# A whole down projection in three passes of fp32r, contiguous expert down weights, and pad slots left out of the scatter-add

## The chip, the cores and the metric

The kernel runs on one core of one Trainium2 chip. The metric is the device time of one execution in microseconds (us); the profile is one profiled execution.

## The reference

One layer of a streaming encoder in float32, over 1024 prompt tokens and 64 sample tokens (N = 1088 rows of width D = 1024):

```python
h   = rmsnorm(x, g0) * (1 + sc_m) + sh_m          # adaLN modulation from c @ w_ada
mix = concat(pool_mixer(u), window_attention(q, k, v)) @ w_out
x   = x + gt_m * rmsnorm(mix, g1)
h   = rmsnorm(x, g2) * (1 + sc_f) + sh_f
# 64 experts of width 256, each token goes to 6 of them, weighted
y   = sum_e w_e * ((silu(h @ w_gate[e]) * (h @ w_up[e])) @ w_down[e])
y  += (silu(h @ ws_gate) * (h @ ws_up)) @ ws_down # shared expert
x   = x + gt_f * rmsnorm(y, g3)
```

The outputs are x and the last rows of the pooling, key and value states.

## The kernel before

The first 560 us do the mixing sub-layer, the shared expert and the routing. The routing gives each expert a list of slots, cut into tiles of 128 slots; the last tile of an expert is filled up with pad slots. There are 1088 x 6 = 6528 real slots. The run had 83 tiles (each has one `y_of` on ScalarE, L1047) for 64 experts, so 19 tiles are a second tile of an expert; `ftab` marks the first tile of an expert, `etab` names the expert. Below, a tile whose step rounds new weights is called a fresh one.

Every engine walks over the tiles in a loop of its own, written out by hand (`tile(i, odd)`), and they meet at semaphores. What each does in step i:

- **SyncE** loads expert weights into a ring of four slots: gate and up (1 MB each, in two halves) as soon as the last tile of the expert four back has been through gate and up, down (1 MB) as soon as that tile has been through the down projection. It issues gate and up of an expert only after the ones before have landed; the down load of the expert before is then still in flight. A partition's half row of gate or up is 4 KB in one piece, and down is 4 KB rows, two per partition.
- **GpSimd** gathers the rows of h of tile i+3 from `h2_rows` by index (`gather`, L771; pad slots hold the index N + r, which is out of bounds, and are skipped), then adds the weighted results of tile i-1 to `y_acc` in HBM with an accumulating indirect DMA (`scatter_add`, L779). It waits for the scatter-add before it (`added`), since two tiles may hold the same token. Pad slots add into the P spare rows N to N+127 of `y_acc`.
- **ScalarE**: SiLU of the gate (L1062), copy of the transposed x rounded to fp32r (`xt_copy`, L1002), in a fresh tile rounding of the next expert's gate and up to fp32r (`round_next`, L983, two of 128x2048), `y_of(i-1)` (L1047, which also needs `slot_columns`), copy of the transposed activations as plain f32 (`at_copy`, L1042).
- **VectorE**: product of SiLU and up (`act_of`, L1389), what rounding left over of x (`xt_rest`, L1398), three index columns (L1407, L1402, L1403; before L1402 it waits until the scatter-add of tile i-3 has landed), in a fresh tile what rounding left over of gate and up (`rests`, L492, two of 128x2048), written over the raw weights in the ring.
- **TensorE**: transposes of the activations of tile i-1 (`act_t`, L1760, 2 instructions), gate and up of tile i in three passes of fp32r (`expert_in`, L1669 to L1671, 24 matmuls of 512 columns), transposes of x of tile i+1 (`x_t`, L1749, 8), down projection of tile i-1 in plain f32 (`expert_out`, L1770: 4 matmuls of 512 columns, each of which stands as two instructions).

The shared expert already does its down projection in three passes of fp32r with the helper `swiglu_out` (12 matmuls of 512 columns). After the last scatter-add, `y_acc` is read back, normalised, and added.

## Time and profile before

| | |
|---|---|
| time, median of 3 runs | 1466.43 us (1465.84 to 1475.8) |
| profiled execution | 1465.69 us, of which span 1463.9 us |
| mean granted TensorE clock | 0.977 of full speed |
| busy | PE 91%, VectorE 54%, ScalarE 45%, GpSimd 26% |
| moved by DMA | 352.38 MB; queue q1 (SyncE) 279.39, q0 (GpSimd) 72.38 |
| expert stage | from 560 us to the last scatter-add's landing at 1430 us |

The span runs from the first to the last instruction; the profiled execution is 1.8 us longer. q0 carries the gathers and the scatter-adds, q1 the weights. The share of a DMA queue is the time of its packets as a share of 16 DMA engines. "SPq" is SyncE's queue, "PEld" TensorE's weight load. In a timeline a row has the start, the duration, engine, line, operation and, in brackets, the idle time before it and what ended it.

### The profile page before, as it was taken

How to read it: one execution, taken by the hardware profiler on the slowest of the kernel's cores; microseconds unless marked ns; L12 is line 12 of the kernel's file. 1: busy time of each engine (PE TensorE's matmuls, PEld its weight loads, DVE VectorE, ACT ScalarE, POOL GpSimd, SP SyncE). 2: the span in 40 equal slices, each digit the busy share in tenths (PEclk: the TensorE clock that was granted, in tenths of full speed). 3: DMA queues.
4: the chain of work that ended last, by engine and by line, in shares of the span. 5: the costliest groups of instructions: out<-in, count | busy, mean ns of one | idle time of the engine just before them, and what ended most of it. 6: DMA issues, size and time to landing. Idle time of an engine off the chain costs nothing.

```text
span 1463.9 us, 22685 instructions
## 1 busy us (share of the span) xinstructions
PE 1338.2 (91%) x5590; PEld 882.4 (60%) x5591; DVE 794.7 (54%) x1254; ACT 656.7 (45%) x916; POOL 387.2 (26%) x274
## 2 busy tenths in 40 slices
PE   4999997899998989999999999999999999999950
PEld 1467654545455766766666666776667667667630
DVE  2446676835887634555546454465545345555426
ACT  2300005734435335555555454465555345555523
POOL 3000000003565431233333323243222333232330
PEclk9999999999999999999999999999999999999995
DMA  8925424032221626999999999999999989999977
GB/s 303 347 79 184 143 69 120 1 145 86 87 90 42 223 88 227 343 324 322 358 310 307 349 318 358 295 311 326 362 324 317 261 225 275 290 338 322 315 193 254
DMA packets 106744, 352.38 MB, mean 241 GB/s; under 512 B 16369, under 2 KB 18517, under 8 KB 106356
## 3 DMA queue, kind: packets, MB, share of 16 engines
q1 hardware_dynamic: 79864, 279.39, 52.8%
q0 software_dynamic: 26560, 72.38, 21.3%
q8 instruction: 19, 0.31, 0.1%
q10 hardware_dynamic: 284, 0.16, 0.1%
q14 instruction: 17, 0.14, 0.0%
HBM read 307.15 MB, written 62.83 MB: 253 GB/s over the span
## 4 chain that ended last, share of the span: by engine, by line
PE 39%; DMA 37%; DVE 9%; SPq 5%; issue 4%; ACT 3%; POOL 2%; ACTq 0%; POOLq 0%; DVEq 0%
DMA raw<-in_w_up_dram 25%; DMA y_acc<-arena,idxs 8%; PE ps L1529 7%; PE ps L1770 7%; PE ps L1669 4%; PE ps L1671 4%; PE ps L1670 4%; SPq L582 3%; PE ps L1622 3%; DMA arena<-in_w_ada_dram 2%; PE ps L1474 2%; DMA y_acc<-arena 2%; PE ps L1749 2%; SPq L649 1%; PE ps L1534 1%
## 5 line engine op out<-in xcount | busy, mean ns | idle before, releaser
L492 DVE TENSOR_TENSOR lo_ring<-raw,hi_gate_up (+1 forms) x128 | 287.7, 2289 | 166.5 <-ACT hi_gate_up L983 156.6
L1770 PE MATMUL ps<-raw,aT 128*128 x664 | 301.9, 598 | 19.3 <-ACT aT L1042 17.0
L983 ACT ACTIVATE hi_gate_up<-raw (+1 forms) x128 | 238.1, 1908 | 120.4 <-SPq L663 93.5
L779 POOL DMA_INDIRECT y_acc<-arena,idxs x83 | 152.2, 1834 | 522.8 <-DMA y_acc<-arena,idxs 389.6
L1669 PE MATMUL ps<-hi_gate_up,xTh 128*128 x664 | 266.3, 401 | 1.1 <-issue 1.1
L1671 PE MATMUL ps<-hi_gate_up,xTl 128*128 x664 | 259.5, 391 | 0.0
L1670 PE MATMUL ps<-lo_ring,xTh 128*128 x664 | 259.0, 390 | 0.0
L1770 PEld LDWEIGHTS ps<-raw,aT 128*128 128x128 f32 x664 | 120.2, 191 | 142.9 <-issue 142.8
L771 POOL DMA_INDIRECT arena<-h_rows,idxg x86 | 114.8, 1334 | 100.0 <-DVE idxg L1407 77.0
L1671 PEld LDWEIGHTS ps<-hi_gate_up,xTl 128*128 128x128 f32 x664 | 124.7, 188 | 26.9
L1669 PEld LDWEIGHTS ps<-hi_gate_up,xTh 128*128 128x128 f32 x664 | 124.8, 188 | 24.5 <-issue 1.2
L1670 PEld LDWEIGHTS ps<-lo_ring,xTh 128*128 128x128 f32 x664 | 125.0, 188 | 23.7
L1398 DVE TENSOR_TENSOR xTl<-ps,xTh 128x1024 fp32r<-128x1024 f32 x84 | 102.7, 1223 | 66.4 <-ACT xTh L1002 66.2
L1529 PE MATMUL ps<-arena 128*128 128x384 f32 (+1 forms) x432 | 135.8, 476 | 1.1 <-DVE arena L1138 1.1
L1622 PE MATMUL ps<-arena 128*128 128x512 f32 (+1 forms) x288 | 128.4, 601 | 0.5 <-ACT arena L910 0.5
L1389 DVE TENSOR_TENSOR arena<-arena,ps 128x256 f32<-128x256 f32 x83 | 34.8, 419 | 166.7 <-ACT arena L1062 166.6
L1047 ACT ACTIVATE arena<-ps,wcol 128x1024 f32<-128x1024 f32 x83 | 91.3, 1100 | 58.9 <-PE ps L1770 44.3
L1062 ACT ACTIVATE arena<-ps 128x256 f32<-128x256 f32 x82 | 31.4, 383 | 189.4 <-PE ps L1671 189.3
L1529 PEld LDWEIGHTS ps<-arena 128*128 128x128 f32 x432 | 83.2, 193 | 53.0 <-issue 5.0
L750 POOL TENSOR_TENSOR arena<-arena 128x1024 f32<-128x1024 f32 (+1 forms) x9 | 22.0, 2443 | 314.8 <-DVE arena L1305 314.8
L1002 ACT ACTIVATE xTh<-ps 128x1024 fp32r<-128x1024 f32 x84 | 86.1, 1025 | 33.4 <-PE ps L1749 33.3
L1622 PEld LDWEIGHTS ps<-arena 128*128 128x128 f32 (+1 forms) x288 | 52.4, 186 | 65.4 <-issue 64.5
(244 smaller groups left out, 1457.4 us busy)
## 6 DMA issues: line engine op xcount, KB each, us to landing
raw<-in_w_gate_dram SPq DMA_DIRECT2D x128, 512.0 KB, 6.0
raw<-in_w_up_dram SPq DMA_DIRECT2D x128, 512.0 KB, 9.0
raw<-in_w_down_dram SPq DMA_DIRECT2D x64, 1024.0 KB, 11.8
arena<-in_w_ada_dram SPq DMA_DIRECT2D x32, 512.0 KB, 6.4
arena<-in_w_ada_dram SPq DMA_DIRECT2D x4, 2048.0 KB, 17.4
arena<-in_x_prompt_dram SPq DMA_DIRECT2D x16, 512.0 KB, 8.9
x_rows<-arena SPq DMA_DIRECT2D x8, 512.0 KB, 2.9
h_rows<-arena SPq DMA_DIRECT2D x8, 512.0 KB, 2.6
```

Source lines behind the costliest of these rows:

```text
L492: return eng.tensor_tensor(lo_of(e, m), raw_of(e, m), hi_of(e, m).bitcast(F32), ALU.subtract)
L771: pool.indirect_dma_start(out=xg[b], out_offset=None, in_=h2_rows, in_offset=bass.IndirectOffsetOnAxis(ap=idxg[b][:, 0:1], axis=0), bounds ...
L779: pool.indirect_dma_start(out=y_acc, out_offset=bass.IndirectOffsetOnAxis(ap=idxs[b][:, 0:1], axis=0), in_=yw[b], in_offset=None, bounds_c ...
L983: act.activation(hi_of(e, m), raw_of(e, m), ACT.Copy).then_inc(round_gu, 1)
L1047: act.activation(yw[b], pair(2), ACT.Copy, scale=wcol[b][:, 0:1]).then_inc(yw_s, 1)
L1398: dve.tensor_tensor(xTl, pair(6).rearrange("p (k n) -> p k n", k=KD), xTh.bitcast(F32), ALU.subtract)\
L1529: ins = pe.matmul(out[:, 0:n_], w1[:, k, P * c:P * (c + 1)], hT[:, k, a:a + n_], start=(k == 0), stop=(k == KD - 1))
L1622: ins = pe.matmul(bank(2 * (t % 2) + half)[0:ROWS[t], :], hT[:, k, P * t:P * t + ROWS[t]], wo[:, k, 512 * half:512 * half + 512], start=(k ...
L1669: pe.matmul(out, at_h[:, k, :], w_h, start=first, stop=False)
L1670: pe.matmul(out, at_h[:, k, :], w_l, start=False, stop=False)
L1671: return pe.matmul(out, at_l[:, k, :], w_h, start=False, stop=last)
L1770: ins = pe.matmul(bank(2 + half), aT[:, k, :], down[:, k, 512 * half:512 * half + 512], start=(k == 0), stop=(k == KF - 1))
```

## The change

Four things: the down weights are loaded as (p k) n, so that a partition holds rows 2p and 2p+1 in 8 KB without a break, and `act_of` writes its columns in the matching order (a step of two elements in both of its inputs); ScalarE rounds the down weights (`round_down`, one 128x2048 per expert, one expert ahead, behind `at_copy`) and VectorE makes their rest (`down_rest`) and the rest of the activations (`act_rest`, 128x256); `expert_out` is `swiglu_out` with 12 matmuls of fp32r and waits for both rests; the scatter-add skips indices from N on and `y_acc` keeps 2 spare rows, which two small copies at the start touch instead of 128. The semaphores of the last reads are merged with earlier ones.

```diff
-        down_v = w_down[0].rearrange("e (k p) n -> e p k n", p=P)
+        down_v = w_down[0].rearrange("e (p k) n -> e p (k n)", k=KF)
...
-            for r in (0, P // 2):
-                pool.dma_start(y_acc[N + r:N + r + P // 2, :], x_prompt[0, r:r + P // 2, :]).then_inc(added, 16)
+            for r in range(2):
+                pool.dma_start(y_acc[N + r:N + r + 1, :], x_prompt[0, r:r + 1, :]).then_inc(added, 16)
...
-                                        in_=yw[b], in_offset=None, bounds_check=add_bound,
+                                        in_=yw[b], in_offset=None, bounds_check=row_bound, oob_is_err=False,
                                         compute_op=ALU.add).then_inc(added, 16)
...
             def at_copy(i):
                 act.wait_ge(at_mm, i + 1)
-                act.activation(aT, bank(5)[:, 0:DE]..., ACT.Copy).then_inc(at_s, 1)
+                act.activation(aTh, bank(5)[:, 0:DE]..., ACT.Copy).then_inc(aeh_s, 1)
+
+            def round_down(e):
+                act.wait_ge(dn_ready, e + 1)
+                act.activation(hi_of(e, 2), raw_of(e, 2), ACT.Copy).then_inc(round_dn, 1)
+
+            def round_next_down(i):
+                f = act.value_load(ftab[0:1, bass.ds(i, 1)], min_val=0, max_val=2)
+                e = act.value_load(etab[0:1, bass.ds(i, 1)], min_val=0, max_val=NE - 1)
+                with act.If(f > 1):
+                    round_down(e + 1)
...
+            act.wait_ge(shg_mm, NT)
+            round_down(0)
             round_next(0)
             at_copy(0)
+            round_down(1)
...
                 y_of(i - 1, 1 - odd)
                 at_copy(i)
+                round_next_down(i)
...
             def act_of(i):
                 dve.wait_ge(silu_s, i + 1)
-                dve.tensor_tensor(act_m, sg, bank(4)[:, DE:2 * DE], ALU.mult).then_inc(act_s, 1)
+                def of_k(x):
+                    return x.rearrange("p (q k) -> p k q", k=KF)
+                dve.tensor_tensor(act_m.rearrange("p (k q) -> p k q", k=KF), of_k(sg), of_k(bank(4)[:, DE:2 * DE]), ALU.mult)\
+                    .then_inc(act_s, 1)
...
+            def down_rest(e):
+                dve.wait_ge(round_dn, e + 1)
+                dve.tensor_tensor(lo_of(e, 2), raw_of(e, 2), hi_of(e, 2).bitcast(F32), ALU.subtract)\
+                    .then_inc(lo_dn, 1)
...
+            def act_rest(i):
+                dve.wait_ge(aeh_s, i + 1)
+                dve.tensor_tensor(aTl, bank(5)[:, 0:DE]..., aTh.bitcast(F32), ALU.subtract)\
+                    .then_inc(ael_s, 1)
...
                 slot_columns(i - 1, 1 - odd)
                 rests(i)
+                act_rest(i)
+                next_down_rest(i)
...
             def expert_out(i, e):
                 pe.wait_ge(yw_s, i + 1)
-                pe.wait_ge(dn_ready, e + 1)
-                pe.wait_ge(at_s, i + 1)
-                down = raw_of(e, 2).rearrange("p (k n) -> p k n", k=KF)
-                for half in range(2):
-                    for k in range(KF):
-                        ins = pe.matmul(bank(2 + half), aT[:, k, :], down[:, k, 512 * half:512 * half + 512],
-                                        start=(k == 0), stop=(k == KF - 1))
-                ins.then_inc(dn_mm, 1)
+                pe.wait_ge(lo_dn, e + 1)
+                pe.wait_ge(ael_s, i + 1)
+                swiglu_out(2, aTh, aTl, hi_of(e, 2), lo_of(e, 2)).then_inc(dn_mm, 1)
```

## Rows read from the trace of the kernel before

**Rows 1.** Page of the profile, part 1: busy time, share of the span, instructions
```profile
PE 1338.2 (91%) x5590; PEld 882.4 (60%) x5591; DVE 794.7 (54%) x1254; ACT 656.7 (45%) x916; POOL 387.2 (26%) x274
```

**Rows 2.** Windows: us; busy (x count) PE PEld DVE ACT POOL; PEclk; DMA share; GB/s
```profile
560.00:1033.00 473.00, 455.37 (x1901) 318.25 (x1899) 245.83 (x299) 256.12 (x254) 148.35 (x89) 1.00 0.98 321
1033.00:1404.00 371.00, 369.88 (x1546) 259.29 (x1547) 181.99 (x236) 193.12 (x199) 110.82 (x74) 1.00 0.95 301
```

**Rows 3.** Waits, 570 to 1404 us: who waited for what, us, times, longest
```profile
POOL y_acc L779 <- DMA y_acc<-arena,idxs: 375.4, 59, 8.8
...
ACT hi_gate_up L983 <- SPq L663: 93.5, 25, 6.7
```

**Rows 4.** Timeline of TensorE: one expert tile, then the shared expert's down projection
```profile
1073.72 3.60 PE L1770 MATMUL ps<-raw,aT 128*128 x8
1077.15 0.38 PE L1760 MATMUL ps<-ident,arena 128*128 128x128 f32 x2
...
539.99 0.39 PE L1669 MATMUL ps<-hi_down,aTsh 128*128 128x512 f32 x1
...
542.48 0.39 PE L1671 MATMUL ps<-hi_down,aTsl 128*128 128x512 f32 x1
```

**Rows 5.** Timeline of ScalarE in a tile that rounds new weights
```profile
1085.59 3.72 ACT L983 ACTIVATE hi_gate_up<-raw  x2 [0.65 <-issue]
1089.22 1.09 ACT L1047 ACTIVATE arena<-ps,wcol 128x1024 f32<-128x1024 f32 x1
1090.21 0.37 ACT L1042 ACTIVATE aT<-ps 128x256 f32<-128x256 f32 x1
```

**Rows 6.** Timeline of VectorE in the same tile
```profile
1083.47 0.42 DVE L1389 TENSOR_TENSOR arena<-arena,ps 128x256 f32<-128x256 f32 x1 [7.09 <-ACT arena L1062]
1084.98 1.23 DVE L1398 TENSOR_TENSOR xTl<-ps,xTh 128x1024 fp32r<-128x1024 f32 x1 [1.09 <-ACT xTh L1002]
...
1086.24 0.14 DVE L1403 COPY idxs<-prod 128x1 int32 x1
1087.96 4.50 DVE L492 TENSOR_TENSOR lo_ring<-raw,hi_gate_up  x2 [1.57 <-ACT hi_gate_up L983]
1093.55 0.42 DVE L1389 TENSOR_TENSOR arena<-arena,ps 128x256 f32<-128x256 f32 x1 [1.09 <-ACT arena L1062]
```

**Rows 7.** Timeline of ScalarE behind a late weight load
```profile
611.36 0.37 ACT L1042 ACTIVATE aT<-ps 128x256 f32<-128x256 f32 x1
...
611.88 1.03 ACT L1002 ACTIVATE xTh<-ps 128x1024 fp32r<-128x1024 f32 x1
```

**Rows 8.** DMA queues (packets, MB, share): 317:318.5, 313.8:315.8, 961.5:962.3 twice, 1424:1430.5
```profile
q1 hardware_dynamic: 155, 0.62, 100.4%
...
q1 hardware_dynamic: 117, 0.86, 102.4%
...
DMA packets 51, 0.14 MB, mean 169 GB/s; under 512 B 18, under 2 KB 18, under 8 KB 51
...
q0 software_dynamic: 51, 0.14, 42.5%
...
q0 software_dynamic: 144, 0.52, 52.4%
```

**Rows 9.** Timeline of GpSimd's scatter-adds (loaded; weight queue silent; tail), and ScalarE's last
```profile
1055.41 1.57 POOL L779 DMA_INDIRECT y_acc<-arena,idxs  x1 [7.16 <-DMA y_acc<-arena,idxs]
...
1065.54 1.58 POOL L779 DMA_INDIRECT y_acc<-arena,idxs  x1 [7.22 <-DMA y_acc<-arena,idxs]
...
1389.78 1.58 POOL L779 DMA_INDIRECT y_acc<-arena,idxs  x1 [5.54 <-DMA y_acc<-arena,idxs]
...
1396.72 1.57 POOL L779 DMA_INDIRECT y_acc<-arena,idxs  x1 [2.27 <-DMA y_acc<-arena,idxs]
...
1424.03 1.55 POOL L779 DMA_INDIRECT y_acc<-arena,idxs  x1 [5.64 <-issue]
...
1416.59 1.11 ACT L1047 ACTIVATE arena<-ps,wcol 128x1024 f32<-128x1024 f32 x1 [6.18 <-DVE idxs L1403]
```

More of the change, by code:

```diff
@@ L98, in build @@
         slot_rows = nc.dram_tensor("slot_rows", (NE * CAP, 2), F32, kind="Internal").ap()
-        y_acc = nc.dram_tensor("y_acc", (N + P, D), F32, kind="Internal").ap()
+        y_acc = nc.dram_tensor("y_acc", (N + 2, D), F32, kind="Internal").ap()
         BIG, TR, XS, RW = RING * WSLOT, KD * N, NT * D, 4 * 2 * D
@@ L168, in build @@
         xTh, xTl = f32r_tiles("xTh", BIG + 6 * D, KD), f32r_tiles("xTl", BIG + 7 * D, KD)
-        aT = nc.alloc_sbuf_tensor_at("aT", [P, DE], F32, offset=SBUF_AT + 4 * (BIG + 5 * D + 2 * DE))[:, :]\
-            .rearrange("p (k n) -> p k n", k=KF)
+        aTh, aTl = f32r_tiles("aTh", BIG + TR + XS + 3 * D, KF), f32r_tiles("aTl", BIG + TR + XS + 3 * D + DE, KF)
         def at(a, n):
@@ L391, in build @@
         at_mm = sem("at_mm")
-        at_s = sem("at_s")
         slot_col = sem("slot_col")
@@ L396, in build @@
         added = sem("added")
-        y_in = [sem(f"y_in{t}") for t in range(NT)]
+        aeh_s = sem("aeh_s")
+        ael_s = sem("ael_s")
+        round_dn = sem("round_dn")
+        lo_dn = sem("lo_dn")
         fin_ss = sem("fin_ss")
@@ L584, in load_down @@
             def load_down(g, s):
-                src = down_v.rearrange("(g s) p k n -> s g p k n", s=RING)[s, bass.ds(g, 1)].rearrange("a p k n -> (a p) k n")
-                sp.dma_start(raw_at(2, (s + 1) % RING).rearrange("p (k n) -> p k n", k=KF), src).then_inc(dn_slot[s], 16)
+                src = down_v.rearrange("(g s) p n -> s g p n", s=RING)[s, bass.ds(g, 1)].rearrange("a p n -> (a p) n")
+                sp.dma_start(raw_at(2, (s + 1) % RING), src).then_inc(dn_slot[s], 16)
             def load_expert(g, s):
@@ L672, in _ @@
                     sp.wait_ge(dn_mm, last_of + 1)
-                sp.dma_start(x1_t(t)[0:ROWS[t], :], x1_rows[P * t:P * t + ROWS[t], :]).then_inc(y_in[t], 16)
+                sp.dma_start(x1_t(t)[0:ROWS[t], :], x1_rows[P * t:P * t + ROWS[t], :]).then_inc(x_in[t], 16)
             last = sp.value_load(lasti[0:1, NE - 1:NE], min_val=NE - 1, max_val=MAX_TILES - 1)
@@ L676, in _ @@
             for t in range(NT):
-                sp.dma_start(y_t(t)[0:ROWS[t], :], y_acc[P * t:P * t + ROWS[t], :]).then_inc(y_in[t], 16)
+                sp.dma_start(y_t(t)[0:ROWS[t], :], y_acc[P * t:P * t + ROWS[t], :]).then_inc(x_in[t], 16)
             for t in range(NT):
@@ L763, in _ @@
                 scatter_slots(t, 0, TOPK)
-            gather_bound, add_bound = pool.to_reg(N - 1), pool.to_reg(N + P - 1)
+            row_bound = pool.to_reg(N - 1)
             def gather(i, b):
@@ L772, in gather @@
                                         in_offset=bass.IndirectOffsetOnAxis(ap=idxg[b][:, 0:1], axis=0),
-                                        bounds_check=gather_bound, oob_is_err=False).then_inc(gathered[b], 16)
+                                        bounds_check=row_bound, oob_is_err=False).then_inc(gathered[b], 16)
             def scatter_add(i, b):
@@ L1041, in at_copy @@
                 act.wait_ge(at_mm, i + 1)
-                act.activation(aT, bank(5)[:, 0:DE].rearrange("p (k n) -> p k n", k=KF), ACT.Copy).then_inc(at_s, 1)
+                act.activation(aTh, bank(5)[:, 0:DE].rearrange("p (k n) -> p k n", k=KF), ACT.Copy).then_inc(aeh_s, 1)
+            def round_down(e):
[6 more added lines that the diff above has]
+                    round_down(e + 1)
             def y_of(i, b):
@@ L1073, in _ @@
                     r = slice(0, ROWS[t])
-                    act.wait_ge(y_in[t], 32)
+                    act.wait_ge(x_in[t], 64)
                     ins = act.activation(pair(4)[r, :], y_t(t)[r, :], ACT.Square, accum_out=ss3[r, t:t + 1])
@@ L1426, in _, with next_down_rest @@
             rests(0)
+            def down_rest(e):
+                dve.wait_ge(round_dn, e + 1)
+                dve.tensor_tensor(lo_of(e, 2), raw_of(e, 2), hi_of(e, 2).bitcast(F32), ALU.subtract)\
+                    .then_inc(lo_dn, 1)
+            def next_down_rest(i):
+                f = dve.value_load(ftab[0:1, bass.ds(i, 1)], min_val=0, max_val=2)
+                e = dve.value_load(etab[0:1, bass.ds(i, 1)], min_val=0, max_val=NE - 1)
+                with dve.If(f > 1):
+                    down_rest(e + 1)
+            def act_rest(i):
+                dve.wait_ge(aeh_s, i + 1)
+                dve.tensor_tensor(aTl, bank(5)[:, 0:DE].rearrange("p (k n) -> p k n", k=KF), aTh.bitcast(F32), ALU.subtract)\
+                    .then_inc(ael_s, 1)
+            down_rest(0)
+            act_rest(0)
+            down_rest(1)
             def tile(i, odd):
```

## The prediction

> **What bounds the kernel now.** I read the page first [rows 1]: TensorE is busy for 91% of the span and no other engine for more than 60%. That is an average, so I cut the expert stage in two by windows [rows 2]. The reader is to see two things: in both stretches TensorE is nearly always busy (455 of 473 us, 370 of 371), and in both the 16 DMA engines are too (0.98 and 0.95). By the 82 SiLUs of the stage, the first from 560 to 1404 us, a tile takes 10.0 us when nothing is late, as from 1083.47 to 1093.55 on VectorE [rows 6]: 62 of them do. The rest, nearly all before 1033 us, are late by 1 to 3.5 us each, 24 us in all, behind a weight load that hasn't landed: ScalarE waited 93.5 us for one, most of that hidden in the tile [rows 3]. So TensorE sets the pace, and DMA nearly does. A third thing nearly does: GpSimd waits 375 us for the scatter-add before [rows 3]. Beside a busy weight queue one scatter-add follows the other after 10.1 us; where the weight queue is silent, after 6.9 us [rows 9]. At the end that chain alone is what is left: `y_of` of the last tile waits 6.2 us for index columns that wait for a scatter-add, and the last scatter-add is issued at 1424.0, 7.4 us after `y_of` began [rows 9].
>
> **TensorE, removed and added.** The down projection in f32 takes 1077.15 - 1073.72 = 3.43 us; the shared expert's, the same 12 matmuls that come now, goes from 539.99 to 542.48 plus one pitch of 0.23, 2.72 us [rows 4]. Each tile gets 0.71 us shorter on TensorE: 10.0 becomes 9.3. If TensorE were the only bound, 83 x 0.71 = 59 us would come back.
>
> **ScalarE, added.** One rounding of 128x2048 per expert, half of 3.72 = 1.86 us [rows 5], and a second pair of register loads with a branch. In a fresh tile the engine's own work, back to back, is: two roundings 1089.22 - 1085.59 = 3.63, `y_of` 0.99 [rows 5], `at_copy` and SiLU together 0.52, `xt_copy` 1.03 [rows 7], the gap before the rounding 0.65 [rows 5], new rounding 1.86: 8.7 us. The new register loads cost nothing if the sequencer runs them ahead, behind `y_of`; if not, up to the 1.7 us from the last index copy to the next rest on VectorE, which hold the same kind of loads [rows 6]. So 8.7 to 10.4 us. Behind `round_down` SiLU of the next tile is queued, and TensorE's next transposes wait for that.
>
> **VectorE, added.** One rest of 128x2048, half of 4.50 = 2.25 us, and `act_rest`, 0.42 us as the product of the same shape. The fresh tile was 0.42 + 1.14 + 0.12 + 4.5 = about 6.2 us [rows 6] and becomes 8.9 us; with both gaps for register loads (1.5 and 1.3 us, each the 1.7 us less what runs in it) 11.7 us. Behind `down_rest` stand `act_of` and `xt_rest`, for which TensorE waits. Where these engines are late, TensorE's loop is SiLU, 2.25 us for `down_rest`, 0.4, 1.2 for `xt_rest`, 5.5 for gate and up, about 9.4 us. I take 9.6 us for the fresh tile: on TensorE its sequencer hides two such register loads wholly (0 us between 1073.72 + 3.43 and 1077.15, [rows 4]), and behind a late load ScalarE goes over its loop's end without a gap, 0.52 us for two operations [rows 7]. The bounds stay 9.3 and 11.7. The stride of `act_of` I take at 0 to 0.2 us, hidden in the same way. In the Trainium skill, SBUF - State Buffer, section Door 1, a step of two fp32 leaves two hits per 16-byte line in SBUF but breaks PSUM's 8-byte lines; no row here shows a VectorE read of PSUM with that step, and 0.2 us per tile would be 17 us only if VectorE were the bound.
>
> **Weight loads.** A 4 KB packet takes 1.004 x 1.5 x 16 / 151 = 0.160 us (151 of the 155 packets), an 8 KB packet 1.024 x 2 x 16 / 105 = 0.312 us (0.86 MB is 105 of them) [rows 8]. Down becomes 8 packets of 0.312 per engine instead of 16 of 0.160: 0.06 us per expert, 4 us over 64, and only where DMA is the bound. The skill's Perfetto Trace Analysis, DMA Optimizations, says that going from 2 to 4 or 8 KB "can dramatically improve throughput"; by these two rows it doesn't from 4 to 8, and by the rule the case with free DMA below would be the forecast.
>
> **The pad slots.** 83 x 128 - 6528 = 4096 of 10624 rows, 38%, leave the scatter-add. A 4 KB packet of it took 0.524 x 6.5 x 16 / 128 = 0.43 us in the last one, alone in the engines [rows 8]; spread evenly, 49 rows less would free 49 x 0.43 / 16 = 1.3 us of 11.4 per tile. But what does leaving out slots do? The gathers show it, which skip pads already. Where one with pads was alone in the engines its packets held 42.5% of them, and 18 of the 51 packets were under 512 B [rows 8]: a skipped row still passes as a tiny packet, and the real rows sit on about half of the engines, as those with the low partitions. The skill's DMA: Bandwidth & Descriptors, section The descriptor swizzle, puts partitions 0 to 63 on engines 0 to 7, eight each; the 42.5% agrees. A scatter-add has landed when its fullest engine is done, and a weight load too. So with 64 rows or more the busier half of the engines keeps all its work; only tiles with few rows gain, mostly some of the 19 second tiles, about half of the data phase, which is 8 packets x 0.43 = 3.4 us (the rest of the 10.1 is issue, queueing and landing). Bounds: nothing, and 38% of 3.4 = 1.3 us off every scatter-add. I take the low end, to which the row with 42.5% is nearer: 10.1 us for most tiles, 8.4 for a dozen, 9.8 on the mean beside a busy weight queue, less where it falls silent.
>
> **The sum, against the profiled execution of 1465.7 us.** First stretch, 473 us, 45 tiles: its limit is now DMA's fuller half. 38 experts x 0.06 = 2 us, 4 few-row tiles x 1.7 = 7, and 5, an estimate of 1%, for packets that share memory with fewer: -14 us. Bounds: -2, and 37 tiles at 9.5 with 8 at 9.3 = 426, -47. Second stretch, 371 us, 37 tiles: the pace is the latest of TensorE 9.3, fresh tiles 9.6, scatter chain 9.6 (9.8 with some silence): 37 x 0.4 = -15 us. Bounds: 9.3 for all, -26; 25 fresh tiles at 10.6, halfway up, with 12 at 9.3, +6. Tail: the last scatter-add could be issued at 1414.2 if `y_of` of tile 82 weren't waiting; of these 10 us I take half, -5 (0 to -10). Start: two roundings and two rests ahead of tile 1, 2 x 1.86 + 2 x 2.25 = 8 us on two engines, mostly behind the first loads: +3 (0 to +8). The small copies to spare rows at 6 us into the run, semaphores and the 9 loads at the end: 0, nobody waits for them. Sum -31: 1434.7. The profiled execution is 0.7 us under the median, so 1435.
>
> **Rivals.** *The row count counts everywhere* (DMA and scatter chain both come free): then compute sets the pace, 426 + 37 x 9.5 = 778 instead of 844, tail -10, start +3: about 1393 at best; with some late loads left, 1405. For it: 38% fewer rows and 17 MB less to move, with DMA at 0.98. Against it: the 42.5%. *Nothing comes free*: skipped rows leave the chain at 10.1 us and the first stretch at DMA's pace, so TensorE only waits more; tail and 8 KB packets alone: -6, about 1460. For it: a third of the tiles already waits for DMA and the chain was at 10.1 beside TensorE's 10.0. Against: the chain falls to 6.9 us whenever weights pause, and a late load is partly made good behind a second tile. *VectorE becomes the bound* (the other side): its fresh tile has 8.9 us of work and register loads with 0 to 2.8 us of gaps. From 10.0 us on it costs more than TensorE gives. With all gaps but a little, 11.0: 64 x 11.0 + 19 x 9.3 = 881 instead of 844, less 5 for late loads that it hides and 5 at the tail: about 1493. For it: the gap of 1.72 us is there in each fresh tile [rows 6], and VectorE must wait for ScalarE's `round_down` on top. Against: at 1087.96 VectorE was idle anyway, so the gap doesn't show what a full queue does.
>
> **How the numbers follow.** Forecast (1435, its own range 1418 to 1450) 0.50; row count counts everywhere (1405) 0.16; nothing comes free (1460) 0.18; VectorE (1493) 0.16. A measurement of this kernel tells about 1%, 15 us, from no change. Faster by over 1% (under 1451.8): 0.50 x 0.95 and 0.16 and a little of the third: 0.65. Slower by over 1% (over 1481): 0.13, the VectorE case at over 10.6 us. Same: the rest, 0.22. The range cuts half of the last case and some of the first rival: 1400 to 1482.
>
> **What would show it.** Twelve fp32r matmuls at a pitch of 0.23 us in place of L1770. Fresh tiles near 9.6 us by the SiLUs, second tiles near 9.3, and still some near 11 us before 1033. VectorE's idle time before `act_of` gone, and before `down_rest` a wait for `round_down`. Gaps named "issue" on VectorE of over 1 us in each fresh tile would speak for the last rival. Scatter-adds at 10 us beside the weights, unless their tile has few rows, with tiny packets in place of the pads: if all land in under 8 us, the first rival holds. The forecast fails most simply if the late weight loads of the first stretch vanish, or if SiLU to SiLU exceeds 10.0 us.

## The result, and the profile after

The changed kernel takes 1474.85 us (median of 20 runs, 1464.81 to 1483.59) against 1466.37 us (20 runs, 1460.29 to 1475.8): a ratio of 1.0052, 95% interval 1.0034 to 1.0069. I had forecast 1435. The profiled span is 1476.8 us, 12.9 us more than before.

The page, part 1 (busy time) and part 4 (the chain that ended last), beside [rows 1]: TensorE is busy for 26 us less (the records of its matmuls overlap and their ends are modelled, so this isn't 83 times the gain of a tile), VectorE for 168 us more. The last line is part 4 of the kernel before: the scatter-add was 8% of its chain and is 26% now, and the weight loads (`raw<-in_w_up_dram`) went from 25% to 10%.

```profile
PE 1311.9 (89%) x5922; PEld 950.4 (64%) x5923; DVE 963.2 (65%) x1401; ACT 777.2 (53%) x980; POOL 420.7 (28%) x274
...
DMA y_acc<-arena,idxs 26%; DMA raw<-in_w_up_dram 10%; PE ps L1573 7%; PE ps L1713 5%; PE ps L1714 5%; PE ps L1715 5%; PE ps L1666 3%; DMA arena<-in_w_ada_dram 2%; SPq L545 2%; DMA y_acc<-arena 2%; SPq L583 2%; PE ps L1793 1%; PE ps L1578 1%; PE ps L1548 1%; POOL arena L751 1%
...
DMA raw<-in_w_up_dram 25%; DMA y_acc<-arena,idxs 8%; PE ps L1529 7%; PE ps L1770 7%; PE ps L1669 4%; PE ps L1671 4%; PE ps L1670 4%; SPq L582 3%; PE ps L1622 3%; DMA arena<-in_w_ada_dram 2%; PE ps L1474 2%; DMA y_acc<-arena 2%; PE ps L1749 2%; SPq L649 1%; PE ps L1534 1%
```

Windows by stretch, columns as in [rows 2]. Where TensorE was busy for 455 of 473 us it is busy for 427, in the second for 357 of 373, and the DMA share fell from 0.98 and 0.95 to 0.90 and 0.87. The two that set the pace before, TensorE and DMA, are less busy, and nothing got shorter: the time sits in waits.

```profile
560.00:1033.00 473.00, 427.02 (x2006) 343.06 (x2004) 330.25 (x365) 315.75 (x281) 160.08 (x87) 0.99 0.90 297
1046.00:1419.00 373.00, 356.51 (x1698) 288.39 (x1697) 252.28 (x301) 242.60 (x225) 128.36 (x74) 1.00 0.87 281
```

The waits of the expert stage, beside [rows 3]. GpSimd still waits mostly for the scatter-add before. Its wait in L772, the gather, for an index column from VectorE went from 58 to 138 us. The wait of ScalarE for weights (L984) has more than halved, from 93.5 us, so late weights are not the loss. TensorE waits 41 us ahead of the down projection for the rest of the activations (`aTl`), which the change has added; before, it waited there for 17 us for `aT`.

```profile
POOL y_acc L780 <- DMA y_acc<-arena,idxs: 288.5, 52, 9.9
POOL arena L772 <- DVE idxg L1427: 137.7, 41, 8.5
...
ACT arena L1060 <- DVE idxs L1423: 43.2, 14, 6.4
...
PE ps L1713 <- DVE aTl L1463: 41.2, 28, 5.1
...
ACT hi_gate_up L984 <- SPq L664: 40.2, 13, 5.1
...
DVE wcol L1422 <- DMA y_acc<-arena,idxs: 30.6, 20, 4.6
```

TensorE's own part came out nearly as forecast: in its timeline the twelve fp32r matmuls of a down projection follow at 0.23 us, but the first takes 0.33, and so does the step to the transposes behind the last. From the first matmul to what follows is 2.86 us on the median of the tiles, against 3.44 before ([rows 4] had 3.43): 0.58 us less, where I had put 0.71.

```profile
1076.45 0.50 PE L1713 MATMUL ps<-hi_down,aTh 128*128 x1
1076.78 0.40 PE L1714 MATMUL ps<-lo_ring,aTh 128*128 x1
...
1079.06 0.39 PE L1715 MATMUL ps<-hi_down,aTl 128*128 x1
1079.38 0.44 PE L1804 MATMUL ps<-ident,arena 128*128 128x128 f32 x2
```

A tile with nothing late now takes 9.3 to 9.4 us instead of 10.0, and 29 of the 82 intervals from SiLU to SiLU are under 9.6 us (one was before). But 29 are over 10.8 (15 before), and the mean went from 10.30 to 10.52. The chain, cut to one window, shows what such tiles wait for: one scatter-add after the other, each piece from its issue to its landing (columns: start, us, what).

```profile
1034.00 10.27 DMA y_acc<-arena,idxs
...
1045.11 11.38 DMA y_acc<-arena,idxs
...
1057.33 11.62 DMA y_acc<-arena,idxs
...
1069.78 10.41 DMA y_acc<-arena,idxs
```

The 12.9 us by stage, from SiLU times and the last rows, beside what I had put in the sum: start, to the first SiLU, 559.9 to 556.7: -3 (forecast +3). First 45 tiles, 473.3 to 489.6: +16 (forecast -14). The other 37, 371.0 to 373.0: +2 (forecast -15). From the last SiLU to the issue of the last scatter-add, 19.8 to 17.6: -2 (forecast -5). The last `y_of` and the last scatter-add, beside [rows 9]:

```profile
1434.89 1.11 ACT L1060 ACTIVATE arena<-ps,wcol 128x1024 f32<-128x1024 f32 x1 [8.51 <-DVE idxs L1423]
...
1436.81 1.55 POOL L780 DMA_INDIRECT y_acc<-arena,idxs  x1 [5.39 <-ACT arena L1060]
```

### The profile page after: what moved, and what is told of

Its sections match the earlier page's. It is cut to its first block, busy times and chain, and to the rows that moved or that the text cites. A ratio compares the mean times of both kernels' runs of the same rounds, so it can differ in the third digit from the quotient of the medians.

```text
span 1476.8 us, 25947 instructions
## 1 busy us (share of the span) xinstructions
PE 1311.9 (89%) x5922; PEld 950.4 (64%) x5923; DVE 963.2 (65%) x1401; ACT 777.2 (53%) x980; POOL 420.7 (28%) x274
## 4 chain that ended last, share of the span: by engine, by line
DMA 41%; PE 32%; DVE 10%; issue 6%; SPq 4%; ACT 3%; POOL 2%; DVEq 1%; ACTq 1%; POOLq 0%
DMA y_acc<-arena,idxs 26%; DMA raw<-in_w_up_dram 10%; PE ps L1573 7%; PE ps L1713 5%; PE ps L1714 5%; PE ps L1715 5%; PE ps L1666 3%; DMA arena<-in_w_ada_dram 2%; SPq L545 2%; DMA y_acc<-arena 2%; SPq L583 2%; PE ps L1793 1%; PE ps L1578 1%; PE ps L1548 1%; POOL arena L751 1%
## 5 line engine op out<-in xcount | busy, mean ns | idle before, releaser
L493 DVE TENSOR_TENSOR lo_ring<-raw,hi_gate_up (+1 forms) x128 | 287.7, 2289 | 119.4 <-ACT hi_gate_up L984 89.3
L780 POOL DMA_INDIRECT y_acc<-arena,idxs x83 | 161.8, 1949 | 424.5 <-DMA y_acc<-arena,idxs 300.2
L984 ACT ACTIVATE hi_gate_up<-raw (+1 forms) x128 | 238.1, 1909 | 74.0 <-SPq L664 40.2
L772 POOL DMA_INDIRECT arena<-h_rows,idxg x86 | 139.2, 1618 | 179.1 <-DVE idxg L1427 156.9
L1713 PE MATMUL ps<-hi_down,aTh 128*128 x332 | 141.0, 425 | 43.0 <-DVE aTl L1463 42.5
L1450 DVE TENSOR_TENSOR lo_ring<-raw,hi_down (+1 forms) x64 | 146.5, 2289 | 49.1 <-ACT hi_down L1047 48.5
L1714 PE MATMUL ps<-lo_ring,aTh 128*128 x332 | 133.2, 401 | 0.0
L1715 PE MATMUL ps<-hi_down,aTl 128*128 x332 | 133.0, 401 | 0.0
L1047 ACT ACTIVATE hi_down<-raw (+1 forms) x64 | 122.6, 1916 | 13.6 <-issue 13.3
L1713 PEld LDWEIGHTS ps<-hi_down,aTh 128*128 128x128 f32 x332 | 64.2, 193 | 64.1 <-issue 52.7
## 6 DMA issues: line engine op xcount, KB each, us to landing
raw<-in_w_down_dram SPq DMA_DIRECT2D x64, 1024.0 KB, 10.8
arena<-in_w_ada_dram SPq DMA_DIRECT2D x4, 2048.0 KB, 17.6
```

The lines of the kernel that those rows point to most:

```text
L493: return eng.tensor_tensor(lo_of(e, m), raw_of(e, m), hi_of(e, m).bitcast(F32), ALU.subtract)
L772: pool.indirect_dma_start(out=xg[b], out_offset=None, in_=h2_rows, in_offset=bass.IndirectOffsetOnAxis(ap=idxg[b][:, 0:1], axis=0), bounds ...
L780: pool.indirect_dma_start(out=y_acc, out_offset=bass.IndirectOffsetOnAxis(ap=idxs[b][:, 0:1], axis=0), in_=yw[b], in_offset=None, bounds_c ...
L984: act.activation(hi_of(e, m), raw_of(e, m), ACT.Copy).then_inc(round_gu, 1)
L1047: act.activation(hi_of(e, 2), raw_of(e, 2), ACT.Copy).then_inc(round_dn, 1)
L1450: dve.tensor_tensor(lo_of(e, 2), raw_of(e, 2), hi_of(e, 2).bitcast(F32), ALU.subtract)\
```

## The experiments

Ratios are to the kernel before on the same chip, with the 95% interval. Not all runs were made on one chip, so between two changed versions the ratios compare better than the medians. Where a landing time of scatter-adds is given, it is counted in the packet records: from the issue to the end of the last packet of that scatter-add, for some 80 of them in a run.

### One part of the change at a time

**Pad slots alone**, on the kernel before.

```diff
-                                        in_=yw[b], in_offset=None, bounds_check=add_bound,
+                                        in_=yw[b], in_offset=None, bounds_check=gather_bound, oob_is_err=False,
```

> The kernel before with one part of the change alone: the scatter-add leaves the pad slots out. If a scatter-add lands when its fullest DMA engine is done, only the tiles with few rows gain: 1455 us (1448 to 1464). If rows count wherever they are, the late weight loads (24 us) and the backlog at the end (10 us) go: 1432. If it does nothing: 1466.

Measured: 1457.51 us, 0.9942 (0.992 to 0.9963).

**Pad slots back**, on the changed kernel (the reverse edit).

> The changed kernel with the pad slots back in the scatter-add. If VectorE sets the pace (its own work and the gap before the rests, 11.2 us per fresh tile), nothing changes: 1475 us. If the chain of scatter-adds sets it, or DMA does, it gets slower by what the pads cost: 1485 to 1500.

Measured: 1479.95 us, 1.01 (1.0066 to 1.0135). The two agree: the pad slots are worth 0.5 to 0.6%, 7 to 9 us, and aren't where the loss is. In the packet records of the changed kernel the data phase of a scatter-add (from its first data packet to its last) takes 2.9 us with up to 35 real rows (13 tiles), 4.6 with 36 to 64, 4.9 with all 128; in the kernel before, where all have 128, it takes 4.6. Only few-row tiles gain, as forecast.

**8 KB packets alone**, on the kernel before, with the activation's permuted order.

```diff
-        down_v = w_down[0].rearrange("e (k p) n -> e p k n", p=P)
+        down_v = w_down[0].rearrange("e (p k) n -> e p (k n)", k=KF)
```

> The kernel before with one part of the change alone: the down weights load with 8 KB to a partition instead of 4 KB, and the product of the activation is written in the permuted order that this layout needs. The transfer of an expert's down weights is 2 to 3% of its own time shorter. If the weight queue sets the pace, that is some 0.06 us for each of 64 experts, 4 us in all: 1461 us. If the chain of scatter-adds sets it, the packets are at most a change of the traffic beside it: 1463 to 1466 us, no difference.

Measured: 1482.61 us, 1.0103 (1.0064 to 1.0143). This is the one part of the change that I had booked as a gain without a doubt, and it costs 15 us by itself. The permuted product isn't it: it takes 418 ns a time, 419 before. In the waits of this run GpSimd's for the scatter-add is longer than in [rows 3], and VectorE's (L1405, ahead of the index columns) is 135 us where it was 21 before, while ScalarE's for weights fell to 43.5. So the weights came earlier and the scatter-adds later, and part 4 of the page (the last line below) says the same: the scatter-adds are 40% of the chain that ended last, where they were 8%, and the weight loads 2% for 25%. The order of the rows in memory changed with the packets here; the runs on packets below keep it fixed.

```profile
POOL y_acc L779 <- DMA y_acc<-arena,idxs: 410.9, 65, 10.1
...
DVE wcol L1405 <- DMA y_acc<-arena,idxs: 135.1, 51, 7.2
...
ACT arena L1047 <- DVE idxs L1406: 85.1, 24, 8.3
...
ACT hi_gate_up L983 <- SPq L663: 43.5, 15, 6.7
...
DMA y_acc<-arena,idxs 40%; PE ps L1532 7%; PE ps L1773 4%; PE ps L1672 3%; PE ps L1674 3%; PE ps L1673 3%; PE ps L1625 3%; DMA raw<-in_w_up_dram 2%; DMA arena<-in_w_ada_dram 2%; PE ps L1477 2%; DMA y_acc<-arena 2%; PE ps L1752 1%; PE ps L1537 1%; PE ps L1507 1%; POOL arena L750 1%
```

### Is the scatter-add the bound?

**A thin scatter-add**: 128 of the 1024 columns, into a tensor of its own; on the changed kernel and on the one before.

```diff
-                pool.indirect_dma_start(out=y_acc, out_offset=...,
-                                        in_=yw[b], ...
+                pool.indirect_dma_start(out=y_thin, out_offset=...,
+                                        in_=yw[b][:, 0:P], ...
```

> The changed kernel, but the scatter-add adds only 128 of 1024 columns, into a tensor of its own; the other 7/8 of the experts' results are left out. DMA has 23 MB less to move and the chain gets short. If VectorE sets the pace (11.2 us where it is never idle), most of the time stays: 1455 us or more. If the scatter-add chain or DMA sets it, tiles fall to TensorE's 9.3 us: 1405 us.

> The kernel before with the same thin scatter-add (7/8 of the experts' results left out). TensorE's 10.0 us per tile stays, the late weight loads and the backlog at the end go: 1430 us under every theory; if it stays at 1460, neither cost what was read from the trace.

Measured: 1409.28 us, 0.9611 (0.9575 to 0.9646), and 1431.86 us, 0.9772 (0.9736 to 0.9807). With the scatter-add out of the way the changed kernel is 22.6 us faster than the one before (the whole change, 8 KB packets and late register loads with it). The three passes are a gain that something in the scatter-add's neighbourhood eats. It isn't VectorE's own work: that is all there in the first of the two runs, and a tile takes 9.7 us on the mean.

**Two accumulators**: odd tiles add into a tensor of their own, so two scatter-adds are in flight with every byte still moved; changed kernel, then kernel before.

```diff
-                pool.wait_ge(added, 16 * (i + 2))
+                pool.wait_ge(added[b], 8 * (i - b) + 16)
...
-                pool.indirect_dma_start(out=y_acc, ...
+                pool.indirect_dma_start(out=y_odd if b else y_acc, ...
```

> The changed kernel with two accumulators and two chains: the odd tiles add into a tensor of their own, each scatter-add waits only for the one two tiles before it, so that two are in flight. The kernel's end reads the even tiles' tensor alone, so the odd tiles' results are left out of the output, and nothing is added for them. Every byte is still moved. Theory (the chain of scatter-adds, one in flight at a time, sets the pace): the tile falls to what TensorE, VectorE and the weight queue allow, as with the thin scatter-add or a little above it, 9.7 to 10.1 us in place of 10.5: 1410 to 1440 us. Rival (the weight queue or the load of the DMA engines as a whole sets the pace): the same bytes take the same time, 1465 to 1475 us.

> The same edit on the kernel before: two accumulators, two scatter-adds in flight, the odd tiles' results left out of the output. TensorE needs 10.0 us for a tile here. Theory: the tile falls from 10.3 to about 10.05 us, 20 us in all: 1440 to 1450 us, so that the change seen without the chain is worth 10 to 25 us by the difference to the run above. Rival (the load of the DMA engines): 1460 to 1466 us.

Measured: 1455.49 us, 0.9925 (0.9898 to 0.9953), and 1450.99 us, 0.9903 (0.9864 to 0.9941). The order of the scatter-adds costs 19 us in the changed kernel and 16 in the one before, less than I expected in the first; the other 46 us between the changed kernel's run and its thin one come with the bytes, not with the order. My theory (the chain alone) fell by that part. GpSimd's wait for a scatter-add is gone here and stands at the gather instead:

```profile
POOL arena L774 <- DVE idxg L1429: 334.0, 82, 9.1
```

### VectorE and the register loads

VectorE, with a down rest in the tile, runs through without a pause but one. Its timeline in the changed kernel, beside [rows 6]: from `act_of` to `act_of` 11.2 us, of which 1.9 stand before the rests (L493), where the register loads are; the trace names ScalarE's rounding there, as [rows 6] did, but the first of those two roundings started at 1078.05 and took 1.9 us, so it was done 2.5 us before the rest began.

```profile
1078.22 0.41 DVE L1408 TENSOR_TENSOR arena<-arena,ps 128x256 f32<-128x256 f32 x1
1078.55 1.22 DVE L1418 TENSOR_TENSOR xTl<-ps,xTh 128x1024 fp32r<-128x1024 f32 x1
1079.68 0.15 DVE L1427 COPY idxg<-prod 128x1 int32 x1
1080.31 0.15 DVE L1422 COPY wcol<-maskb 128x1 f32 x1 [0.48 <-DMA y_acc<-arena,idxs]
1080.44 0.15 DVE L1423 COPY idxs<-prod 128x1 int32 x1
1082.48 4.49 DVE L493 TENSOR_TENSOR lo_ring<-raw,hi_gate_up  x2 [1.89 <-ACT hi_gate_up L984]
1086.89 0.42 DVE L1463 TENSOR_TENSOR aTl<-ps,aTh 128x256 fp32r<-128x256 f32 x1
1087.22 2.28 DVE L1450 TENSOR_TENSOR lo_ring<-raw,hi_down  x1
1089.42 0.41 DVE L1408 TENSOR_TENSOR arena<-arena,ps 128x256 f32<-128x256 f32 x1
```

**No down rest**: VectorE doesn't make it, and TensorE's second pass reads the rounded weights in its place.

```diff
-                next_down_rest(i)
...
-                swiglu_out(2, aTh, aTl, hi_of(e, 2), lo_of(e, 2)).then_inc(dn_mm, 1)
+                swiglu_out(2, aTh, aTl, hi_of(e, 2), hi_of(e, 2)).then_inc(dn_mm, 1)
```

> The changed kernel without down_rest on VectorE (2.25 us per expert less): TensorE still makes 12 fp32r matmuls, but the pass with the rest of the down weights takes the rounded weights again, so the result lacks that correction. If VectorE's own work, in the way of the scatter-adds or alone, makes fresh tiles long: 1445 us. If the scatter-add chain alone sets the pace: 1470.

Measured: 1468.36 us, 1.0029 (1.0004 to 1.0054): 2.29 us of VectorE's work for each of 64 experts, 146 us, are worth 3 us by the ratios, 6 by the medians. The interval overlaps that of the changed kernel (1.0034 to 1.0069), so even this isn't clear of noise.

**Register loads at the head of the tile**, on VectorE and ScalarE.

```diff
             def tile(i, odd):
+                f, e = dve_flags(i)
                 act_of(i)
                 xt_rest(i + 1)
...
-                rests(i)
+                rests(f, e)
```

> The changed kernel with the register loads (ftab, etab) for round_next and rests at the head of the tile on ScalarE and VectorE, so that they run while the engine has work. If the gap of 1.7 to 2 us before the rests lies on the path in fresh tiles, about half of 62 x 1.8 us comes back: 1430 us (1415 to 1445). If the scatter-add chain sets the pace whatever VectorE does: 1470 or more.

Measured: 1466.86 us, 1.0008 (0.9988 to 1.0029), 0.44% under the changed kernel, 6 us by the ratios and 8 by the medians; the two intervals just miss each other. Taken as it stands, this is at least as much as all of the down rest. In the trace the gap before the rests, where the loads had stood, falls from 1.9 us to 0.47 where VectorE waits for nothing else:

```profile
757.07 4.49 DVE L493 TENSOR_TENSOR lo_ring<-raw,hi_gate_up  x2 [0.47 <-issue]
```

**The wait for the scatter-add off VectorE** (GpSimd copies the indices itself, and ScalarE waits for the scatter-add of tile i-3 ahead of `y_of` in VectorE's place), and this with the early register loads.

```diff
                 pool.wait_ge(added, 16 * (i + 2))
+                pool.tensor_copy(idxs[b][:, 0:1], itab[:, bass.ds(i, 1)]).then_inc(pidx_s, 1)
+                pool.wait_ge(pidx_s, i + 1)
```

> The changed kernel with the wait for the scatter-add of tile i-3 taken off VectorE: GpSimd copies the scatter indices itself, ScalarE waits before y_of. VectorE's rests are no longer behind a scatter-add. If it is the coupling of both (a late scatter-add holds VectorE, whose work then holds the next gather and scatter-add): 1450 us. If VectorE alone: 1473. If the chain of scatter-adds alone: 1475 or slower by the copy on GpSimd.

> Flags first and wait moved together. If the two stand in one loop, the gains add to what is left by the scatter-adds and the weight loads: 1425 us. If the flags alone matter, as with flags first; if neither, 1475.

Measured: 1492.12 us, 1.0171 (1.0117 to 1.0225), and 1478.31 us, 1.0084 (1.0063 to 1.0106): no gain, and of the cases named only "slower by the copy on GpSimd" is left. The timeline of GpSimd in the first shows such a cost: a copy (0.2 us on the median, up to 2.3) and up to 0.85 us more now stand between the landing of one scatter-add and the issue of the next; on the median that step went from 1.3 to 1.7 us. But the edit also put a wait on ScalarE, 118 us in 35 times, and no run parts the two.

```profile
1049.02 2.11 POOL L779 COPY idxs<-prod 128x1 int32 x1 [4.97 <-DMA y_acc<-arena,idxs]
1051.98 1.60 POOL L783 DMA_INDIRECT y_acc<-arena,idxs  x1 [0.85 <-PE ps L1796]
...
1060.06 0.18 POOL L779 COPY idxs<-prod 128x1 int32 x1 [4.07 <-DMA y_acc<-arena,idxs]
1061.08 1.60 POOL L783 DMA_INDIRECT y_acc<-arena,idxs  x1 [0.84 <-ACT arena L1064]
```

**GpSimd's order turned round**: scatter-add of tile i-1 first, then the gather of tile i+3.

```diff
-                pool.wait_ge(xt_mm, i + 2)
-                gather(i + AHEAD, 1 - odd)
                 scatter_add(i - 1, 1 - odd)
+                pool.wait_ge(xt_mm, i + 2)
+                gather(i + AHEAD, 1 - odd)
```

> The changed kernel with GpSimd's order in a tile turned round: the scatter-add of tile i - 1 is issued ahead of the gather of tile i + 3, so that a late index column from VectorE (the gather's wait for it is 138 us in 41 waits of the changed kernel, 58 us in the one before) no longer holds the scatter-add. Theory: VectorE's added work reaches the time by way of that gather; the chain then starts its links earlier by 1 to 2 us in the tiles where VectorE is late, 5 to 20 us in all: 1455 to 1468 us. Rival: the scatter-add waits for the one before it anyway and the gather's wait lies inside that: 1474 us, no change. Second rival: the gathers come later by the tail of the down projection and TensorE waits for its rows: 1480 us or more.

Measured: 1518.79 us, 1.0369 (1.0329 to 1.0409). The second rival holds, and by far: GpSimd now waits for `y_of` with the gather behind it, and TensorE's transposes of x (L1793) wait for the gathers, which in the kernel before they did for less than 3 us in all.

```profile
POOL y_acc L780 <- ACT arena L1060: 273.1, 39, 12.8
...
PEld ps L1793 <- DMA arena<-h_rows,idxg: 72.8, 40, 4.3
PE ps L1793 <- DMA arena<-h_rows,idxg: 56.4, 35, 3.9
```

### The packets

**4 KB transfers in the changed kernel**: two DMAs for an expert's down weights instead of one; the layout, the arithmetic and the permuted product stay.

```diff
-                sp.dma_start(raw_at(2, (s + 1) % RING), src).then_inc(dn_slot[s], 16)
+                for q in range(2):
+                    part = slice(MAT // 2 * q, MAT // 2 * (q + 1))
+                    sp.dma_start(raw_at(2, (s + 1) % RING)[:, part], src[:, part]).then_inc(dn_slot[s], 16)
```

> The changed kernel with the down weights of an expert loaded in two transfers of 4 KB to a partition in place of one of 8 KB; the layout, the arithmetic and the bytes are those of the change. Theory (a 4 KB packet of the scatter-add waits behind weight packets twice as long, and the chain of scatter-adds sets the pace): the 15 us that the packets alone cost the kernel before come back, 1474.9 - 15 = 1460 us, range 1455 to 1465. Rival (the 8 KB part cost something by its address order or by the activation's permuted write, both of which stay): 1475 us, no change. Second rival (VectorE's lateness alone holds the chain): 1470 to 1475 us.

Measured: 1454.29 us, 0.9908 (0.9875 to 0.994). The theory holds and was too small: 21 us come back, and the kernel is faster than before. A transfer is half as long here too, but in the run with 8 KB alone one transfer had stayed one transfer, so the packets are what both have in common. Its waits, beside those of the changed kernel above: ScalarE waits longer for weights again (63 us for 40), and VectorE less for the scatter-add (12 for 31).

```profile
POOL y_acc L782 <- DMA y_acc<-arena,idxs: 319.3, 59, 8.1
POOL arena L774 <- DVE idxg L1429: 112.5, 50, 8.9
...
ACT hi_gate_up L986 <- SPq L666: 63.2, 21, 5.6
...
DVE wcol L1424 <- DMA y_acc<-arena,idxs: 12.1, 7, 6.9
```

**8 KB for gate and up** in the kernel before, nothing else changed.

```diff
-                    for h in range(2):
-                        part = slice(MAT // 2 * h, MAT // 2 * (h + 1))
-                        sp.dma_start(raw_at(m, (s + 1) % RING)[:, part], src[:, part]).then_inc(gu_slot[s], 16)
+                    sp.dma_start(raw_at(m, (s + 1) % RING), src).then_inc(gu_slot[s], 16)
```

> The kernel before with the gate and the up weights of an expert loaded in one transfer of 8 KB to a partition each, in place of two of 4 KB; nothing else is changed, neither the layout nor the arithmetic nor the activation's order. Two thirds of the weights' bytes change packet size, where the run with the down weights alone changed one third and cost 1.0%. Theory (weight packets twice as long beside the scatter-add): 1.5 to 2.5% slower, 1488 to 1503 us. Rival (the packet size is harmless, the down weights' layout did it): 1463 to 1468 us.

Measured: 1475.11 us, 1.0065 (1.0038 to 1.0092). Slower, by packets alone, without any change of layout; but by 10 us and not by 22 to 37. The cost isn't in proportion to the bytes that change. In the chain that ended last the scatter-adds are 44%.

```profile
POOL y_acc L777 <- DMA y_acc<-arena,idxs: 401.7, 66, 9.0
...
DVE wcol L1400 <- DMA y_acc<-arena,idxs: 104.0, 38, 5.5
...
ACT hi_gate_up L981 <- SPq L661: 16.7, 7, 4.5
```

**4 KB transfers and early register loads together**; then 4 KB transfers with two accumulators.

> The version above with the register loads of VectorE and ScalarE at the head of a tile, which alone took the changed kernel from 1474.9 to 1466.9 us. Theory: both repairs act on the same loop and add up in most part, 1460 - 5 to 8 = 1452 to 1455 us, which is below the kernel before by 0.8 to 1%. Rival (they are two ways to the same slack, and the second brings nothing): 1460 us.

> The version with 4 KB transfers and two accumulators, two scatter-adds in flight; the odd tiles' results are left out of the output. With 8 KB packets the same edit gave 1455.5 us, and 1451.0 us on the kernel before. Theory (the packets take their toll by the DMA side, TensorE's gain is there once the chain is doubled): 1435 to 1445 us, under the 1451 of the kernel before with two chains. Rival (VectorE's work is what is left): 1455 us.

Measured: 1447.4 us, 0.9876 (0.9839 to 0.9912), and 1450.89 us, 0.9881 (0.9836 to 0.9925). The first is the fastest whole kernel of this study, 1.2% under the one before; its interval overlaps that of the 4 KB run, so what the early register loads add to it is less sure than that both together beat the kernel before. The second expectation failed: once the packets are short, a second scatter-add in flight brings only 3 us against the 4 KB run.

This gives the packets' price with one and with two scatter-adds in flight. With one, 8 KB for 4 KB costs 21 us (1454.3 to 1474.9, ratios 0.9908 to 1.0052). With two it costs 5 to 7 (1450.9 to 1455.5, ratios 0.9881 to 0.9925), which is within the noise. So most of the price is paid through the order: a scatter-add that lands late holds the next one only where the next must wait for it.

**2 KB transfers**, for the down weights and for all three matrices, both with early register loads.

> The version with 4 KB transfers and early register loads (1447 us), with the down weights in four transfers of 2 KB to a partition. If shorter weight packets let the scatter-add through sooner at no price: 1440 to 1446 us. Rival (a 2 KB packet moves fewer bytes in a unit of time, so the weight queue is busy for longer and the scatter-add has no quieter neighbour): at or over the 4 KB version, 1447 to 1460 us.

> As the run with 2 KB for the down weights, and the gate and up weights in 2 KB pieces too, all three matrices in twelve transfers for an expert. It adds what that run shows up to three times over: if 2 KB helps there, 1430 to 1442 us; if it costs, 1455 to 1480 us. The issuing queue also gets 12 transfers for an expert in place of 6, which nothing here has tried.

Measured: 1453.66 us, 0.9931 (0.9908 to 0.9954), and 1458.84 us, 0.9957 (0.9934 to 0.998). Shorter still doesn't help: 4 KB is the best of the three sizes here, though the intervals of the first of these runs and the 4 KB one just touch. The loss comes from the other side now: ScalarE's waits for late weights are 68, 74 and 79 us with 4 KB, 2 KB for down and 2 KB for all, and in the last run the chain that ended last has 29% weight loads and the scatter-add isn't among its largest parts.

The runs of this group side by side. Counted in the packet records: the median packet takes 84 ns at 2 KB, 159 at 4 KB, 309 at 8 KB; a 4 KB packet of the scatter-add 327.

| kernel | scatter-adds that landed after 10.5 us | mean from one issue to the next | scatter-adds / weight loads in the chain that ended last | time, us | ratio |
|---|---|---|---|---|---|
| before, 4 KB | 5 of 82 | 10.30 us | 8% / 25% | 1466.4 | 1 |
| before, gate and up 8 KB | 13 of 82 | 10.40 | 44% / none listed | 1475.1 | 1.0065 |
| before, down 8 KB | 23 of 82 | 10.51 | 40% / 2% | 1482.6 | 1.0103 |
| changed, down 8 KB | 23 of 81 | 10.50 | 26% / 10% | 1474.9 | 1.0052 |
| the same, pad slots back | 14 of 83 | 10.50 | 48% / 3% | 1480.0 | 1.01 |
| changed, down 4 KB | 14 of 80 | 10.17 | 25% / 19% | 1454.3 | 0.9908 |
| with early register loads, 4 KB | 8 of 81 | 10.08 | 25% / 17% | 1447.4 | 0.9876 |
| the same, down 2 KB | 14 of 80 | 10.17 | 2% / 24% | 1453.7 | 0.9931 |

The count of late landings goes with the packet size on each kernel, but it isn't a measure of the time: with the pad slots back it is 14, and that kernel is slower than the one with 23.

## Why the prediction was wrong

**The step that failed: "Weight loads".** I priced the 8 KB packets by the weight queue's own time, 0.06 us per expert, -4 us, and put their effect on the scatter-adds beside them at nothing. They cost 15 us on the kernel before and 21 us in the changed one; without them the change is at 0.9908. That is 19 to 25 of the 40 us between forecast and measurement. The mean landing of the scatter-adds beside which the weight queue held over 40% of the engines went from 9.2 to 9.4 us on the kernel before, and from 9.0 to 9.5 in the changed one (4 KB, then 8 KB); the late ones multiplied (table); and the price mostly vanishes where two scatter-adds are in flight. By the Trainium skill, Perfetto Trace Analysis, section DMA Optimizations, going from 2 to 4 or 8 KB can improve throughput a great deal; here the step from 4 to 8 KB gained the packets 3% by themselves (309 ns against 2 x 159) and the kernel lost. The skill's Trainium Kernel Development and Optimization, section Key Constraints, says that DMAs of all queues run on the same 16 engines and interleave; that agrees with the later scatter-adds, and I hadn't drawn the consequence. That a scatter-add's packets queue behind longer weight packets is argued from this; the traces here don't show the order inside an engine. What the packet records do show is time beyond the packets' own: in the kernel before a 4 KB packet of a scatter-add takes 0.345 us on the mean (I had 0.43), the 128 of them spread over 16 engines would take 2.8 us, and the data phase is 4.6 us.

**"Scatter chain 9.6 (9.8 with some silence)".** It measured 10.50 from issue to issue, before 10.30. That this equals the tile's mean (10.52 and 10.30) shows nothing by itself, since each tile has one scatter-add. What shows the chain at work is that GpSimd waited for the one before it in 52 tiles of the changed kernel, that the chain that ended last went from 8% to 26% scatter-adds, and that two in flight give 19 us back. In the kernel before it was close to the pace (59 waits, 16 us back with two in flight), but in the chain that ended last there the weight loads were the largest part (25%). I had named it as a third thing that nearly binds and then let it get shorter by the pad slots; it got longer by the packets.

**"I take 9.6 us for the fresh tile", the register loads hidden.** Fresh tiles came at 10.5 to 10.6 us on the mean, by which engine's step is counted, and second tiles, which I had at 9.3, at 10.3 to 10.5. So the loss isn't a matter of the work that only fresh tiles have. Early register loads gave 6 to 8 us back, so the gap wasn't hidden where VectorE is full: the tile in the rows above took 11.2 us, near my upper bound of 11.7. My reason for hiding them was circular: I had taken 3.43 us as the distance from 1073.72 to 1077.15 [rows 4], and then read 0 us of gap between 1073.72 + 3.43 and 1077.15. And the loop of 9.4 us names SiLU but adds only 2.25 + 0.4 + 1.2 + 5.5; with SiLU's 0.4 it is 9.7. But VectorE isn't the bound as the last rival had it: without the whole down rest it is only 3 to 6 us less, and with a thin scatter-add tiles fall to 9.7 us. That its lateness acts by a loop is argued from the waits: a late index column holds the gather (138 us of waits, 58 before), the scatter-add stands behind the gather, and VectorE's next index columns wait for that. Both kinds of edit that were to open this loop made the kernel slower, so no run shows it.

**Right:** the pad slots' low end (only few-row tiles, 8.5 us in all); the stride of `act_of` free (418 ns for 419); late loads of the first stretch fewer but not gone. **Nearly right:** TensorE's gain, 0.58 us per tile for 0.71. I had added one pitch of 0.23 us behind the shared expert's last matmul and missed the slower first one. **Start and tail** were off by 6 and 3 us, with opposite signs. The 5 us in the first stretch "for packets that share memory with fewer" had no row behind them, and no run shows the term; the pad slots by themselves, with whatever they free, gave 8.5 us.

The steps from the kernel before to the changed one, by the ratios (they add up because they are the steps between them): pad slots -0.58%; three passes with early register loads and 4 KB another -0.66% (0.9942 to 0.9876); the late register loads +0.32% (to 0.9908), which is within the noise; the 8 KB packets +1.44% (to 1.0052), which is far outside it. With both repairs the kernel is at 1447, still 12 us above the forecast of 1435.

**Open.** Why the three passes give 10 us beside a full scatter-add (1457.5 to 1447.4) and the change as a whole 23 beside a thin one, with nothing gained where two are in flight (1450.9 at 4 KB, 1451.0 on the kernel before); the DMA engines' load is the candidate (0.92 of the stretch from 560 to 1380 us in the fastest version), and no run took it away without taking the chain too. Also why 8 KB on two thirds of the bytes (0.65%) doesn't cost more than on the last third (1.03%); their intervals overlap, so that it costs less isn't shown.

## What to carry to other kernels

Here the price of a packet size was paid by another queue than the one that was tuned: before making one transfer's packets longer, look for a serial chain of small transfers beside it, and test that part by itself. A gain on the busiest engine shows only as far as the next loop allows, so look for every chain that runs near the tile's pace (here 10.1 us beside 10.0), and ask what your change does to it and not only to the engine that you relieve. Where an engine has become full, look at its gaps for register loads: moving them is a small edit, and on VectorE it gave back 6 to 8 us, where taking 146 us of its work away gave 3 to 6.

## What the hardware did that I hadn't expected

- Packets of 8 KB took 309 ns and two of 4 KB 318, while 2 KB took 84 (168 for 4 KB): 3% and 6%, and yet going from 4 to 8 KB lost 10 to 21 us, and going to 2 KB for the down weights 6 to 8.
- The first data packet of a scatter-add came 4.6 us after its issue beside a busy weight queue, and after 2.1 us where that was silent.
- In the changed kernel a scatter-add of up to 35 real rows had a data phase of 2.9 us, but from 36 rows on it took 4.6 to 5.8 on the mean, and 4.9 with all 128.
- A copy of 128x1 on GpSimd ahead of its own indirect DMA took 0.2 us on the median and up to 2.3, and up to 0.85 us more passed until the issue.
